# Rotary embedding by row copies through DMA instead of products with a rotation matrix, in a two-layer transformer kernel

## The reference

```python
def rmsnorm(x, w):
    y = xf * lax.rsqrt(jnp.mean(xf * xf, axis=-1, keepdims=True) + EPS)
    return (y * w.astype(jnp.float32)).astype(x.dtype)

def apply_rope(x, cos, sin):
    x1, x2 = jnp.split(x.astype(jnp.float32), 2, axis=-1)
    return jnp.concatenate([x1 * c - x2 * s, x2 * c + x1 * s], axis=-1).astype(x.dtype)

    qn = apply_rope(rmsnorm(nq.reshape(B, S, N_HEADS, N_DH), q_norm_w), cos, sin)
    kc_t = to_groups(apply_rope(rmsnorm(kv_heads(kc), kcmp_norm_w), cos, sin))
```

```python
            q = jnp.concatenate([q[..., :MLA_NOPE], apply_rope_2(q[..., MLA_NOPE:], *cs_mla)], axis=-1)
            qd = axial_rope(qd, cs_row, cs_col)
```

## Time and profile before

| | us |
|---|---|
| median of three runs | 2791.16 (2788.06 to 2791.30) |
| the profiled execution's own time | 2786.57 |
| its span in the trace | 2784.7 |

### The profile page before, as it was taken

The page is one execution under the profiler, slowest core; times in us unless marked ns, Lnnn a source line. Parts: engine busy times, 40 slices in busy tenths (PEclk is TensorE's granted clock), DMA queues, the critical chain, the costliest instruction groups (busy, mean ns, idle before and its releaser), DMA issues.

```text
span 2784.7 us, 40601 instructions
## 1 busy us (share of the span) xinstructions
PE 2726.7 (98%) x15808; PEld 2344.3 (84%) x15808; DVE 1820.8 (65%) x2803; ACT 1289.8 (46%) x2192; POOL 517.7 (19%) x514
## 2 busy tenths in 40 slices
PE   8999999999999999999999999999999999999999
PEld 7788778888878898987778999889998787788988
DVE  7677666646467574755867566675756677784755
ACT  5445564323234353543644344543444676653533
POOL 1002232000003121101303212031120344131211
PEclk9999999999999999999999999999999999999999
DMA  4212114222323464531124565354653101234643
GB/s 176 69 61 94 46 34 150 95 93 91 103 87 85 135 171 133 163 106 50 35 95 133 125 171 131 123 140 114 172 133 104 50 20 46 72 103 131 192 118 109
DMA packets 112782, 296.52 MB, mean 106 GB/s; under 512 B 12624, under 2 KB 14672, under 8 KB 112336
## 3 DMA queue, kind: packets, MB, share of 16 engines
q1 hardware_dynamic: 90864, 250.80, 27.4%
q0 software_dynamic: 21152, 42.08, 8.9%
q10 hardware_dynamic: 576, 1.05, 0.1%
HBM read 291.78 MB, written 2.10 MB: 106 GB/s over the span
## 4 chain that ended last, share of the span: by engine, by line
PE 90%; DVE 6%; ACT 2%; issue 1%; POOL 0%; DMA 0%; SPq 0%; ACTq 0%; DVEq 0%; POOLq 0%
PE ps L505 88%; DVE WL L516 2%; PE ps L508 2%; DVE SC L516 1%; ACT HH L513 1%; DVE X L516 1%; ACT WH L513 1%; DVE SC L528 1%; ACT SC L513 0%; DVE HL L528 0%; DMA WF<-wall 0%; POOL SC L523 0%; DVE SM L534 0%; DVE PTL L516 0%; DVE X2v L516 0%
## 5 line engine op out<-in xcount | busy, mean ns | idle before, releaser
L516 DVE TENSOR_TENSOR WL<-WF,WH 128x1024 fp32r<-128x1024 f32 (+4 forms) x625 | 732.4, 1184 | 312.5 <-ACT WH L513 307.9
L513 ACT ACTIVATE WH<-WF 128x1024 fp32r<-128x1024 f32 (+4 forms) x625 | 581.0, 942 | 655.9 <-PE ps L505 621.2
L505 PE MATMUL ps<-HH,WH 128*128 128x512 f32 (+1 forms) x1104 | 441.5, 400 | 16.7 <-DVE HL L528 14.0
L505 PE MATMUL ps<-HH,WL 128*128 128x512 f32 (+1 forms) x1104 | 432.3, 392 | 0.0
L505 PE MATMUL ps<-HL,WH 128*128 128x512 f32 (+1 forms) x1104 | 432.0, 391 | 0.0
L505 PE MATMUL ps<-AH,WH 128*128 128x512 f32 x880 | 344.9, 392 | 19.4 <-DVE WL L516 15.6
L505 PE MATMUL ps<-AL,WH 128*128 128x512 f32 x880 | 342.7, 389 | 0.0
L505 PE MATMUL ps<-AH,WL 128*128 128x512 f32 x880 | 342.5, 389 | 0.0
L505 PE MATMUL ps<-B,WH 128*128 128x256 f32 x1632 | 299.6, 284 | 1.6 <-DVE WL L516 1.4
L516 POOL TENSOR_TENSOR SC<-SC 128x256 f32<-128x256 f32 (+2 forms) x92 | 109.9, 1201 | 966.7 <-DVE SC L528 961.9
L551 POOL DMA_DIRECT2D WF<-wall x136 | 129.4, 960 | 798.4 <-DMA WF<-wall 786.9
(11 more groups left out here) (322 smaller groups left out, 4757.0 us busy)
## 6 DMA issues: line engine op xcount, KB each, us to landing
WF<-wall SPq DMA_DIRECT2D x313, 512.0 KB, 3.7
WF<-wall SPq DMA_DIRECT2D x253, 256.0 KB, 3.0
WF<-wall POOLq DMA_DIRECT2D x136, 256.0 KB, 4.2
WF<-wall SPq DMA_DIRECT2D x40, 384.0 KB, 3.6
X<-xT POOLq DMA_DIRECT2D x8, 256.0 KB, 3.9
outT<-X POOLq DMA_DIRECT2D x8, 256.0 KB, 2.3
WF<-wall SPq DMA_DIRECT2D x4, 288.0 KB, 12.1
LT<-late POOLq DMA_DIRECT2D x1, 1152.0 KB, 5.5
```

What stands on the lines that cost most here:

```text
L505: return self.real.matmul(o, l, r, start=start, stop=stop, skip_group_check=True)
L513: return self.real.activation(o, i, func, bias=bias, scale=scale, accum_out=accum_out)
L516: return self.real.tensor_tensor(o, a, b, op) if self.real is not None else Uncounted()
```

## The change

**The turn.** *rot* is no longer a product. SP copies the rows of y into tile s by DMA, each half of a rotated block to the other half's place; the minus sign of the rotation is now in the tables of sines. `halves_of` gives the copies: 4 of 32 rows for the keys of M, N and D, 8 of 16 rows for gk and gq, 2 of 16 rows for mq and mk0. Tile s is taken at *rot* and no longer at *roped*, the bank of *rot* is gone, and four semaphores are used in rotation, each new turn waiting for the one four before it.

**SP.** The turns stand among the weight pieces in SP's queue. Ahead of a turn, SP issues all weight pieces up to seven beyond the oldest one that isn't split yet by the list at this place.

**DVE and POOL.** The sine product reads tile s instead of a bank. For mq keys it and POOL's add work on the 32 rotated rows alone, and *scaled* then reads y.

**Constants.** The three matrices are gone; cmask and upto come by a DMA of their own into EC, behind the third weight piece.

**Places.** M_TURNS, N_TURNS, D_TURNS, L_TURNS and G_TURNS have new numbers in nearly every row.

```diff
-CONST = (("ident", 128), ("cmask", 128), ("upto", 128), ("ones", 128), ("two", 2),
-         ("r64", 128), ("cos64", S), ("sin64", S), ("cmadd", 124), ("eps", 1))
-LATE = (("r32", 128), ("cosa", S), ("sina", S), ("rm", 128), ("cosm", S), ("sinm", S))
+EARLY = (("cmask", 128), ("upto", 128))
+CONST = (("ident", 128), ("ones", 128), ("two", 2),
+         ("cos64", S), ("sin64", S), ("cmadd", 124), ("eps", 1))
+LATE = (("cosa", S), ("sina", S), ("cosm", S), ("sinm", S))
...
-    c["sin64"] = np.sin(a).T[i % 32]
+    c["sin64"] = turned_sign(32) * np.sin(a).T[i % 32]
...
 M_TURNS = {
...
-    "take": (85, 142, 170, 267, 245),
-    "rot": (91, 173, 211, 265),
...
+    "take": (53, 147, 195, 272, 267),
+    "rot": (61, 148, 196, 280),
...
+def halves_of(ph, key):
+
+    lo, hi, half = (64, 96, 16) if ph == "L" and key[0] == "m" else (0, 128, 16 if key[0] == "g" else 32)
+    out = []
+    for at in range(lo, hi, 2 * half):
+        out += [(slice(at, at + half), slice(at + half, at + 2 * half)), (slice(at + half, at + 2 * half), slice(at, at + half))]
+    return out
...
-SC_TAKES = {"raised": "P", "take": "y", "squares": "sq", "roped": "s", "h_squares": "hq",
+SC_TAKES = {"raised": "P", "take": "y", "squares": "sq", "rot": "s", "h_squares": "hq",
...
+NTURN = 4
...
+            def turn(ph, key):
+                y, to = tile(ph, "y", key), KP if key == "mk0" else tile(ph, "s", key)
+                done, before, _ = turn_of[ph, key]
+                if ph == "L" and key[0] == "m":
+                    e.wait_ge(*copied[ph, "take", key])
+                    if key == "mk0":
+                        e.wait_ge(*stepped[ph, "take", key])
+                else:
+                    e.wait_ge(*emptied[ph, "take", key])
+                if key != "mk0":
+                    for w in tile_left(ph, "s", key):
+                        e.wait_ge(*w)
+                if before:
+                    e.wait_ge(done, before)
+                for o, i in halves_of(ph, key):
+                    e.dma_start(to[o, :], y[i, :]).then_inc(done, 16)
+
+            for phases in ("MN", "D", "LG"):
+                split = [q for ph, stage, key in order[phases] if stage[0] == "w" and stage[-4:] == "_low"
+                         for n in [taken_by(ph, *key)] if n is not None for q in split_after[n]]
+                for ph, stage, key in order[phases]:
+                    if stage == "rot":
+                        if split:
+                            weights(min(split) + NWF)
+                        turn(ph, key)
...
-                elif stage == "rot":
-                    parts, _, _, _, _, rot_ap, _, _ = rope_of(ph, key)
-                    y = tile(ph, "y", key)
...
-                    e.matmul(bank(ph, "rot", key)[0:parts, :], rot_ap, y[0:parts, :], True, True)\
-                     .then_inc(*rotated(ph, "rot", key))
...
                 if stage == "added":
                     parts = rope_of(ph, key)[0]
+                    some = slice(64, 96) if key[0] == "m" else slice(0, parts)
...
-                    e.tensor_tensor(s, s, y, ALU.add).then_inc(*pooled(ph, "added", key))
+                    e.tensor_tensor(y if key[:2] == "mq" else s, s, y, ALU.add).then_inc(*pooled(ph, "added", key))
...
-                    e.wait_ge(*rotated[ph, "rot", key])
-                    for w in tile_left(ph, "s", key):
-                        e.wait_ge(*w)
-                    e.scalar_tensor_tensor(r, bank(ph, "rot", key)[0:parts, :], pc(gain, 1, parts), sin, ALU.mult, ALU.mult)\
+                    e.wait_ge(turn_of[ph, key][0], turn_of[ph, key][2])
+                    turned_gain = pc(gain, 1, 32, 64) if key[0] == "m" else pc(gain, 1, parts)
+                    e.scalar_tensor_tensor(r, r, turned_gain, sin[some, :], ALU.mult, ALU.mult)\
                      .then_inc(*roped(ph, "roped", key))
```

More of the change, by code:

```diff
@@ L184, in constants, with turned_sign @@
     c["two"] = np.stack([i < 64, i >= 64], axis=1).astype(f)
[L186 to L197, removed]
+    def turned_sign(half):
+        return np.where(i % (2 * half) < half, -1.0, 1.0).astype(f)[:, None]
     def angles(pos, dim):
@@ L269 @@
[L269 to L283, removed]
@@ L295 @@
[L295 to L306, removed]
@@ L337 @@
-    "product": (448, 465, 500, 506, 626, 634, 684, 688, 779, 781, 823, 830, 902, 910, 951, 953),
-    "half1": (517, 520, 710, 711, 857, 858, 948, 949),
-    "half2": (545, 546, 713, 728, 864, 866, 946, 947),
-    "parts": (549, 758, 950, 952),
+    "source": (392, 393, 394, 399, 534, 552, 555, 556, 692, 702, 707, 714),
+    "ws_high": (516, 578, 656),
+    "ws_low": (158, 588, 722),
+    "take": (404, 572, 719),
+    "rot": (436, 573, 724),
+    "squares": (446, 563, 734),
+    "roped": (437, 593, 754),
@@ new lines @@
+        126, 158, 159, 160, 188, 190, 195, 197),
+    "ws_high": (5, 149, 45, 39, 79, 110, 152, 206),
+    "ws_low": (1, 140, 34, 52, 96, 104, 162, 222),
+    "take": (8, 22, 27, 43, 84, 107, 157, 207),
+    "rot": (9, 33, 58, 71, 87, 108, 186, 218),
+    "squares": (31, 24, 46, 54, 118, 130, 196, 202),
+    "roped": (26, 37, 81, 72, 109, 143, 194, 224),
+    "added": (32, 60, 78, 89, 103, 145, 189, 247),
+    "sums": (42, 40, 65, 55, 132, 137, 201, 215),
+    "root": (50, 47, 77, 59, 148, 138, 223, 227),
@@ L418 @@
+    "product": (158, 217, 291, 321, 389, 449, 476, 508),
+    "half1": (188, 238, 303, 343, 408, 455, 487, 524),
+    "half2": (211, 244, 317, 350, 416, 451, 485, 527),
+    "parts": (271, 365, 478, 532),
 }
 G_TURNS = {
-    "source": (456, 469, 470, 473, 560, 561, 578, 579, 671, 672, 682, 685),
-    "ws_high": (423, 571, 661),
-    "ws_low": (458, 605, 662),
-    "take": (477, 584, 684),
-    "rot": (507, 586, 697),
-    "squares": (484, 588, 700),
-    "roped": (524, 601, 699),
-    "added": (527, 607, 693),
@@ L451 @@
-    "product": (602, 644, 694, 731, 755, 784, 805, 817),
-    "half1": (606, 632, 702, 737, 764, 785, 813, 822),
-    "half2": (630, 665, 709, 727, 781, 799, 811, 820),
-    "parts": (680, 812, 816, 823),
+    "source": (454, 456, 470, 474, 548, 557, 564, 565, 655, 656, 661, 666),
+    "ws_high": (437, 556, 624),
+    "ws_low": (483, 590, 650),
+    "take": (473, 578, 664),
+    "rot": (521, 579, 665),
+    "squares": (479, 587, 671),
+    "roped": (522, 601, 693),
+    "added": (520, 622, 690),
@@ L455 @@
+    "product": (610, 636, 697, 718, 765, 787, 811, 820),
+    "half1": (619, 647, 702, 734, 776, 786, 810, 818),
+    "half2": (637, 663, 711, 750, 771, 799, 812, 819),
+    "parts": (814, 815, 816, 822),
 }
@@ L961, in sc_takes @@
         return []
-    if ph == "L" and str(key)[:2] == "mk" and stage in ("roped", "scaled"):
+    if ph == "L" and str(key)[:2] == "mk" and stage in ("rot", "scaled"):
         return [(ph, "s", key)] if stage == "scaled" else []
@@ L1158, in build @@
         s_late = sem("s_late")
+        s_turn = [sem(f"s_turn{i}") for i in range(NTURN)]
         s_out = sem("s_out")
@@ L1640, in sync_program, with weights, weight @@
             e.dma_start(PR[:, :], par).then_inc(s_p, 16)
-            for n, (name, _, _, r, c) in enumerate(plan):
+            began = [0]
+            def weights(upto):
+                while began[0] < min(upto, len(plan)):
+                    weight(began[0])
+                    began[0] += 1
+            def weight(n):
+                name, _, _, r, c = plan[n]
                 if n == 1:
```

402 lines of the change are left out of this document (210 added, 192 removed).

## The result

The changed kernel takes 2796.1 us (median of 20 runs, 2792.6 to 2802.3); the kernel before took 2790.6 us beside it (20 runs, 2786.4 to 2794.8). The ratio is 1.0021, with a 95% interval of 1.0014 to 1.0027: slower by 0.2%. I had forecast 2771. The profiled execution took 2793.92 us.

The account below looks back on a forecast made before the run. PE was taken to bound the kernel: -22.9 for the removal, +2 for turns, +0.5 for DVE's sines give -20.4 us, 2766.2 from the profiled 2786.6, or 2771 as median; range 2758 to 2793.

Parts of the forecast that it names:

- Turns +2, up to 8.7: In the mixers, DVE standing for turns not yet landed adds 2 us to the path, from 0 to 8.7.
- What covers it: PE's work between a key's projection end and its roped step covers the turn: 2.7 to 6.4 us for six keys, 7 to 32 for 23.
- SP as the weights' queue: Weight pieces behind a turn wait for its take and tile, but six pieces are under way: nothing added.
- The removal, -22.9: 29 rotations of 0.86 us leave PE in the mixers, 24.9 us; with 92% coming back, -22.9 us.
- 92% of PE time taken out should come back: In the mixers PE bounds; its load waits for no named work are 6.7%, taken as 8%, so 92% returns.
- By stage: Expected savings: M and N 5 to 6 us, D 5 to 7, L and G 9 to 12.
- Landing 1.9 to 3.7 us: A turn's copies within SBUF land in 1.9 to 3.7 us; issue of 4 copies was put at 1.8 us.
- DVE's sine from SBUF: Sine products reading two SBUF tiles take 0.10 us longer each, 2.9 us of DVE, +0.5 on the path; upper end 23 us of DVE.
- New places 0, from -10 to +15: Moving nearly every step in all five tables was taken as 0 us, from -10 to +15.
- C: Rival: DVE becomes the bound in D and in L and G, so -11 us, 2780; chance 0.15.
- D: Rival: the new order gives the gain back, PE's load waits growing from 53 to some 73 us, 2791; chance 0.13.
- E: Rival: turns land late behind weight pieces in SP's queue and DVE stands at roped; at 8 us landing +13.6, 2804; chance 0.10.

Follow-up runs that it names:

- e1: Changed kernel, with SP issuing ahead of a turn only the weight pieces whose buffers are free at the key's take: 2778.6 us, ratio 0.9960 to the kernel before.
- e3: Kernel before, with the 29 rotation products on 8 of 512 columns only, every wait and place kept: 2782.0 us, ratio 0.9976.
- e6: Kernel before, with each rotation product made twice: 2815.1 us, ratio 1.0088.
- e12: As e1, with the turns of G's five keys made by 4 copies of 32 rows in place of 8 of 16: 2779.6 us, ratio 0.9957.
- e8: Kernel before, with the new places in D alone and rotations still products of PE: 2794.8 us, ratio 1.0017 to the kernel before.
- e2: Kernel before, with the turn by DMA in place of the product, steps at their old places (kc's turn 3 steps later): 2831.4 us, ratio 1.0150.
- e9: e1 repeated unchanged, as the base of e10 on the same chip: 2778.0 us, ratio 0.9951 to the kernel before.
- e10: As e1, with two idle fp32 products ahead of L's first projection and one ahead of each of L's first three sums: 2775.1 us, ratio 0.9945.

## Why the prediction was wrong, step by step

- **"Turns +2, up to 8.7": wrong, it was +17, the larger part of the miss.** e1 undoes it in one edit: 10.7 us at full clock and 7.1 of clock. The failed step is in "What covers it": I counted the cover from the end of a key's projection. But SP issues a turn at its place in its queue, behind pieces that wait for DVE's later splits. For nq0, nq1, eq1, mq4 and gq0 this place stands directly ahead of the sine, and these five make 21.1 of the 25.5 us (4.22, 5.07, 4.35, 3.21 and 4.26). In e1 1.1 of these are left. (mq5 and gq1 stand so too, and wait 0.9 us or less.) None of the five is among the six keys that I had named there as the least covered. In "SP as the weights' queue" I had asked what the turn does to the weights, and gave it nothing, and never what the weights do to the turn.
- **The removal, -22.9: its clock was wrong, 8 us.** I had read the clock of 0.99 to 1.00 as given, and no term of the sum has it. By e3 the smaller products take 8.0 us more of clock. The other step, "92% of PE time taken out should come back", was nearly right: 87% in e3 and 88% in e6. From these I estimate 24.9 x 0.87 = 21.7 us at full clock for the whole removal.
- **By stage.** Five waits of PE stand around the mixers in every trace, with the same lengths (1.3 to 2.4 us). They begin, in us from the start:

| wait of PE | before | after | e1 |
|---|---|---|---|
| behind M and N | 437.7 | 441.4 | 432.6 |
| ahead of D | 1176.6 | 1181.4 | 1171.9 |
| behind D | 1428.1 | 1430.1 | 1415.7 |
| ahead of L | 2174.5 | 2175.7 | 2162.4 |
| behind G | 2421.3 | 2426.3 | 2411.7 |

  Up to the first, the changed kernel is 3.7 us longer; around D it is 2.8 shorter, around L and G 3.8 longer. e1 is 5.1 us shorter in M and N and 7.7 in D, about as I had forecast (5 to 6, 5 to 7), but 2.5 longer in L and G, where I had forecast 9 to 12 shorter. There its profiled execution has 17.1 us more at half clock than that of before, so the clock accounts for 8.5 us of it.
- **Landing 1.9 to 3.7 us: right** (2.0). Issue: 4 copies take 2.41 us, not 1.8, since a copy of these takes SP 0.59 us and not 0.48; e12 shows that in e1's order it doesn't matter.
- **DVE's sine from SBUF: right.** Sines and cosines together have means of 746 ns in C and 789 in LT, the products of 32 rows 927, against 735 and 733 from a bank. By count (15, 5 and 8 sines) that is some 2 us of DVE, where I had 2.9; the upper end of 23 us is far off. How much of it reached the path no run shows.
- **New places 0, from -10 to +15: not refuted, and not priced.** The ratio of e1 is 0.0016 below that of e3, 4.5 us. Of these some 5.7 are the 6.6 us of small products that e3 still has, at 87%. So new places, turns in time and sines together cost about 1 us, an estimate. But the places can't be priced apart from the turn: e8 is +5 us, e2 +42.
- **The sum from the runs**: -0.0024 (e3) - 0.0016 (e1 against e3) + 0.0061 (after against e1) = +0.0021, the measured ratio. It meets it by construction, since each ratio stands twice, and is no check; it shows the sizes: 6.7 and 4.5 us gained, 17 lost.
- **Rivals.** C: DVE is at 75 and 80% of D and L/G, under 82%; no. D: the load waits for nothing named went from 44.8 to 47.3 us, far from +20; no. E is the nearest, and I gave it 0.10: SP's queue holds the turn behind pieces and DVE stands. But I had let it decide by the landing, which is short, and argued it away with the pieces' landing and the fixed cost of a DMA. The lateness was there before the DMA began.

## What to carry to other kernels

A transfer has its place in the queue of the engine that issues it: look at what stands ahead of it there and what that waits for, before its size or its landing time. When work leaves the engine that bounds, price the removal by a run that shrinks it in place (e3), and read from its trace what is left of it (here 0.23 of 0.86 us). At full clock this and adding the work once more (e6) gave the same share, 87 and 88%. That they gave 7.5 and 24.2 us in all comes from the smaller amount that e3 takes out, and from the clock. Look also at what the removed work stood between: here it parted rows of small products. Work moved to another mechanism wants its neighbours placed anew: at the old places it cost 42 us.

## What was not expected of the hardware

- PE's clock can halve behind a wait of PE or a row of small products, for 3.4 to 17.1 us at a time. Behind nq0's wait of 3.93 us it was 6.8 us at half (3.4 lost), behind eq1's of 3.51 us 3.4 at half (1.7 lost); behind nq1's and gq0's, 1.19 and 1.71 us, it did not fall, nor behind 2.35 us at L's entry in the kernel before. By the runs' mean clocks the smaller products cost 8.0 us in this way and the late turns 7.1.
- Five idle products in and around a stretch of 12 us kept the clock up for the 17 us behind it (e9 and e10). The Trainium skill's page TensorE: Matmul & The Clock Gate, Part 1: The HAM clock gate, says that the throttled state is the default and activity releases it; e10 against e9 agrees, while e6 had more work on PE than before and a mean clock no higher. It also puts the penalty of the ramp at under 1% of a typical kernel's span. That holds here too (24.9 of 2796.1 us), and yet what the change added to it, 13.2 us, is more than twice the whole difference of 5.5.
- Copies within SBUF of 16 or 32 rows with 2 KB each: 0.51 us of SP for the first issue and 0.59 for each that follows, 2.0 us from issue to landing (median, 1.9 to 3.9), and mostly 1.4 us from the end of the last issue to the last landing.
- A product of DVE with both inputs in SBUF was longer only where an instruction of POOL was under way: of the 15 cosine products of the kernel before, the three that overlap one took 1.00, 1.07 and 1.54 us, the twelve others 0.74.
